# Two steps of ScalarE reordered, the router's product turned the other way, and five clears moved behind the selections, in a two-block transformer kernel

## What is computed

```python
# first block, each layer, after one wide projection of h
qkv_b = jax.nn.silu(causal_depthwise_conv(qkv_b, conv_w[layer]))
q_b, k_b, v_b = jnp.split(qkv_b, ...)
q_b = l2_normalize(q_b.reshape(B, S, GDN_HEADS, GDN_DK))   # x * rsqrt(sum(x*x) + eps)
k_b = l2_normalize(k_b.reshape(B, S, GDN_HEADS, GDN_DK))
o_b = chunked_gated_delta_rule(q_b, k_b, v_b, beta, g)
...
# second block, layer 1, after its attention mixers
c = rms_norm_2(h, norm_ffn[i])
h = h + moe_swiglu(c, moe_router[0], ...)   # logits = c @ router (1024 x 8), 2 of 8 experts a token
gate = jax.nn.sigmoid(rms_norm_2(h, ple_norm[i]) @ ple_w_gate[i])
h = h + (p[i] @ ple_w_proj[i]) * gate
```

## Time and profile before

| | |
|---|---|
| three runs | 2664.57, 2675.79, 2676.34 us; median 2675.79 |
| profiled execution | 2670.33 us, of which the span from first to last instruction is 2668.8 us |
| granted TensorE clock, mean | 0.965 |
| TensorE busy | 2564.6 us, 96% of the span |
| ScalarE busy | 493.8 us, 19% |
| VectorE busy | 637.0 us, 24% |
| read from HBM | 538.12 MB, 202 GB/s over the span |

### The profile page before, as it was taken

How to read it: one execution, slowest core, us unless ns; L and a number is a source line. 1 busy time by engine, 2 the same in 40 slices (tenths; PEclk the granted TensorE clock), 3 DMA queues, 4 the chain that set the end, 5 groups by cost and what they waited for, 6 DMA issues and landing times. The chain is left out here.

```text
span 2668.8 us, 47414 instructions
## 1 busy us (share of the span) xinstructions
PE 2564.6 (96%) x21427; PEld 1435.9 (54%) x21427; DVE 637.0 (24%) x1337; ACT 493.8 (19%) x847; POOL 133.8 (5%) x331
## 2 busy tenths in 40 slices
PE   9999999989999998999999988999999999999998
PEld 8666557756554774444445765353444535353444
DVE  3433532433543532000014443010101001010102
ACT  1521321422322432001013430000000000000001
POOL 4011000011000310000001300000000000000000
PEclk9998998999999988999999888999999999999999
DMA  7421333421335412444346213999999999999991
GB/s 242 130 76 53 111 116 126 142 80 64 105 108 131 147 41 91 142 154 145 134 136 163 82 42 144 370 367 380 356 386 345 375 364 370 373 363 378 358 368 66
DMA packets 192349, 542.29 MB, mean 203 GB/s; under 512 B 29168, under 2 KB 57232, under 8 KB 192144
## 3 DMA queue, kind: packets, MB, share of 16 engines
q1 hardware_dynamic: 178848, 536.95, 55.9%
q10 hardware_dynamic: 12992, 1.22, 0.4%
q0 software_dynamic: 304, 1.05, 0.1%
HBM read 538.12 MB, written 1.05 MB: 202 GB/s over the span
## 5 line engine op out<-in xcount | busy, mean ns | idle before, releaser
L398 PE MATMUL psum<-ring,hT 128*128 128x512 f32 (+3 forms) x1632 | 693.6, 583 | 19.2 <-ACT area L736 13.2
L398 PEld LDWEIGHTS psum<-ring,hT 128*128 128x128 f32 x1632 | 312.3, 199 | 359.7 <-issue 328.1
L2594 PE MATMUL psum<-ring,area 128*32 128x448 f32 x4608 | 439.5, 539 | 1.7 <-DVE area L2767 1.1
L2594 PEld LDWEIGHTS psum<-ring,area 128*32 128x32 f32 x4608 | 149.9, 110 | 283.8 <-issue 281.3
L623 PE MATMUL psum<-hT,ring 128*128 128x256 f32 x768 | 170.6, 385 | 0.0
L623 PEld LDWEIGHTS psum<-hT,ring 128*128 128x128 f32 x768 | 148.8, 194 | 21.7 <-issue 1.0
L2613 PE MATMUL psum<-area 128*32 128x256 f32 x2688 | 149.8, 380 | 2.0 <-ACT area L2743 2.0
L2613 PE MATMUL psum<-ring,area 128*32 128x256 f32 x2688 | 151.5, 380 | 0.0
L2594 PE MATMUL psum<-area 128*32 128x448 f32 x1536 | 147.3, 539 | 0.0
L2613 PEld LDWEIGHTS psum<-area 128*32 128x32 f32 x2688 | 85.7, 110 | 60.2 <-ACT area L2743 3.9
L2613 PEld LDWEIGHTS psum<-ring,area 128*32 128x32 f32 x2688 | 84.9, 110 | 57.1 <-issue 2.9
(11 more groups left out here) (528 smaller groups left out, 2362.7 us busy)
## 6 DMA issues: line engine op xcount, KB each, us to landing
ring<-in_w_in_dram SPq DMA_DIRECT2D x92, 1024.0 KB, 5.1
ring<-in_moe_w_gate_dram SPq DMA_DIRECT2D x96, 896.0 KB, 6.8
ring<-in_moe_w_up_dram SPq DMA_DIRECT2D x96, 896.0 KB, 7.8
area<-in_moe_w_down_dram SPq DMA_DIRECT2D x112, 512.0 KB, 7.4
ring<-in_moe_w_down_dram SPq DMA_DIRECT2D x112, 512.0 KB, 6.9
area<-in_moe_w_gate_dram SPq DMA_DIRECT2D x32, 896.0 KB, 6.7
area<-in_moe_w_up_dram SPq DMA_DIRECT2D x32, 896.0 KB, 8.0
ring<-in_w_out_dram SPq DMA_DIRECT2D x16, 1024.0 KB, 5.0
```

The costliest lines, as they stand in the source:

```text
L398: last = nc.tensor.matmul(acc(g)[:, t, 0:d["n"]], lhs(kk, t), w[:, k, :], start=kk == 0, stop=kk == d["nk"] - 1)
L2594: last = nc.tensor.matmul(PS[32 * j:32 * j + 32, 3 * p + b, 0:PIECE], XG[:, k, 32 * b:32 * b + 32], expert_slot(j0 + j // 2, GROUP * (j % ...
```

## The change

It has three parts, and each has something moved or replaced. `proj1_act` calls `rsqrt(1, p1)`, which copies p1's tile out between Ln and Exp, in both layers of the first block. `pass_act` issues the dummy activation with Sqrt and the read of the count between the last two copies, and `norm_act` leaves its own out for n=8; the branch for the extra passes ends with a Sqrt of its own. In the routing the router's columns are the weights and HT moves through, VectorE copies the 8 x 256 result out, TensorE transposes its two halves, and one copy brings both out; `clear_dve` stands behind the weighed selections.

```diff
-            rsqrt(1)
-            next(p1)
+            rsqrt(1, p1)
             next(p1)
             conv_silu(5)
...
             s.after(...ACT.Ln, bias=eps, scale=scale)...
+                if p1 is not None:
+                    next(p1)
             s.after(...ACT.Exp, scale=-0.5)...
...
+        def root_table(s):
+            s.do(nc.scalar.activation(WARM, ONES[:, 0:1], ACT.Sqrt))
...
-            s.do(nc.scalar.activation(WARM, ONES[:, 0:1], ACT.Sqrt))
+            if n != 8:
+                root_table(s)
...
                 s.after(nc.scalar.activation(PR[:, 0, 0:512], PS[:, 3, :], ACT.Copy)...
+                root_table(s)
+                count = busiest(act)
                 act.wait_ge(sem("weights_used"), used(MOE1))
                 s.after(nc.scalar.activation(PR[:, 1, 0:512], PS[:, 0, :], ACT.Copy)...
+                return count
...
-                for t in range(T):
-                    last = nc.tensor.matmul(PS[:, 2 * t, 0:NE], ht_lhs(k, t), ROUTER[:, k, :],
-                                            start=k == 0, stop=k == KD - 1)
+                last = nc.tensor.matmul(PS[0:NE, 0, 0:S], ROUTER[:, k, :], HT[:, k, :], start=k == 0, stop=k == KD - 1)
+            last.then_inc(signal("moe_rows"), 1)
+            pe.wait_ge(signal("moe_rows_out"), reached("moe_rows_out", 1))
+            for t in range(T):
+                last = nc.tensor.transpose(PS[:, 2, t * NE:(t + 1) * NE], LOGR[:, t * P:(t + 1) * P], IDENT[0:NE, 0:NE])
...
-            clear_dve()
+            s.eng.wait_ge(signal("moe_rows"), reached("moe_rows", 1))
+            s.after(nc.vector.tensor_copy(LOGR, PS[0:NE, 0, 0:S]).then_inc(signal("moe_rows_out"), 1), "moe_rows_out")
             s.eng.wait_ge(signal("moe_logits"), reached("moe_logits", 1))
-            for t in range(T):
-                s.do(nc.vector.tensor_copy(LOGX[:, t, 0:NE], PS[:, 2 * t, 0:NE]))
+            s.do(nc.vector.tensor_copy(LOGX[:, :, 0:NE], PS[:, 2, 0:2 * NE].rearrange("p (t e) -> p t e", t=T)))
...
             ins.then_inc(ms("weighed"), 1)
+            clear_dve()
             s.eng.wait_ge(ms("YE"), 3 + past("YE", r))
```

More of the change, by code:

```diff
@@ L84, in blocks_kernel @@
             "dsa_by_vector": ("dsa_kms", "dsa_roped"),
-            "route_by_vector": ("moe_mask", "moe_shifted", "moe_count"),
-            "route_by_tensor": ("moe_logits", "moe_places"),
+            "route_by_vector": ("moe_rows_out", "moe_mask", "moe_shifted", "moe_count"),
+            "route_by_tensor": ("moe_rows", "moe_logits", "moe_places"),
         }
@@ L649, in conv_silu, with rsqrt @@
                 s.do(nc.scalar.activation(Y[:, 4 * j:4 * j + 4, :], Y[:, 4 * j:4 * j + 4, :], ACT.Silu))
-            def rsqrt(hq):
+            def rsqrt(hq, p1=None):
                 if L + hq == 0:
@@ L2420, in blocks_kernel @@
         IOTA = iota_t[:, 0:CAP]
+        LOGR = view(14728, S)[0:NE]
         MORE = AREA - (MOE_RING - RING * HALF)
@@ L2553, in pass_dve @@
                     s.after(ins.then_inc(ms("placed"), 1), "moe_placed")
-            if r:
-                clear_dve()
-            else:
+            if r == 0:
                 shares_dve(s)
@@ L3061, in _, with second @@
                     s.after(nc.scalar.activation(EXPL, EXPL, ACT.Exp).then_inc(sem("moe_exp"), 1), "moe_exp")
-                    pass_act(s, 0)
-                    overflow(act, lambda: (pass_act(s, 1), pass_act(s, 2)))
+                    count = pass_act(s, 0)
+                    def second():
+                        for r in (1, 2):
+                            pass_act(s, r)
+                        nc.scalar.activation(WARM, ONES[:, 0:1], ACT.Sqrt)
+                    overflow(act, second, count)
                 norm_act(s, n)
```

## The result

The changed kernel takes 2654.78 us (median of 8 runs, 2650.74 to 2660.51), the kernel before 2674.75 (8 runs, 2664.57 to 2676.34). The ratio is 0.9933, 95% interval 0.9917 to 0.9949: faster by 14 to 22 us. The profiled execution of the changed kernel has a span of 2650.0 us against 2668.8, and a mean clock of 0.971 against 0.965.

A forecast was written before the change was run, and what follows sets the result against it. TensorE, busy 96% of the span, was taken as the bound, so time comes from its idle stretches and low clock. Terms of 11.7 + 3.2 + 0.3 = 15.2 us, against a mean of 2671.8, gave 2657 us; range 2647 to 2669.

The forecast's parts named there:

- The copy between Ln and Exp: First projection, both layers: TensorE restarts 3.1 us earlier in each, clock stays up for 5.5 us more; 11.7 us gained.
- Late Exp: First projection: k's product comes later, slack shrinks from 8 to 1.4 us but holds; as rival, 2660 us, chance 0.05.
- The Sqrt table and the count: Last norm: table load and count read leave the path, 2.15 us of wait and 1.0 of clock; 3.2 us gained.
- drain of the table load: Last norm: alternative reading of the 1.25 us ahead of the table load, which would give 2.7 us instead of 2.15.
- The router: Routing: sixteen records of 256 columns take 5.8 us instead of 6.99, less a new round trip; 0.3 us gained.
- The round trip: Routing: new PSUM copy, two transposes and hand-overs cost 0.6 to 1.0 us net, taken as 0.9.
- The place products: Routing: 2.30 us at clock 0.50 could become 1.15 if the clock is up.
- the middle case: Routing: sum of the middle terms, a gain of 0.3 us, between a loss of 0.9 and a gain of 3.6.
- The clears: Routing: 2.2 us of clears now lie in the gather's shadow, still covered, by 0.6 us.
- The clock does not come back: Rival: TensorE restarts earlier in both layers but the clock falls or later stages lose it; 7.5 us, 2664; chance 0.22.
- More than forecast: Rival: clock up through router, places and last norm; 20 us gained, 2652 us; chance 0.10.
- Slower, by the transfers of the experts: Rival: expert transfers fall below 362 GB/s and set the pace; at 3% less, 14 us slower, 2686; chance 0.05.

The follow-up runs named there:

- e1: The kernel before with only the copy of p1's tile moved between Ln and Exp; ratio 0.9950 (0.9932 to 0.9967).
- e5: The kernel before, copy still behind Exp, with four unused products of 512 columns in TensorE's wait for that copy; ratio 0.9980 (0.9968 to 0.9992).
- e2: The changed kernel with the copy of p1's tile back behind Exp; ratio to before 0.9989 (0.9972 to 1.0006).
- e4: The kernel before with only the turned router and the clears behind the selections; ratio 0.9998 (0.9981 to 1.0014).
- e6: The changed kernel with two extra 128x2048 copies on ScalarE between the copy of p1's tile and Exp; ratio to before 0.9974 (0.9959 to 0.9988).
- e8: The changed kernel with unused TensorE products in routing and last-norm waits, and first-pass clears behind the first scaling of gathered tokens; ratio to before 0.9919.
- e3: The kernel before with only the Sqrt table and the read of the count ahead of the last copy; ratio 0.9999 (0.9983 to 1.0016).
- e9: The changed kernel itself, run once more on one chip beside the kernel kept busy in its waits; ratio to before 0.9934, median 2652.99 us.
- e7: The changed kernel with the five clears back ahead of the wait for the router's rows; ratio to before 0.9925 (0.9904 to 0.9946).
- e10: The kernel of e8 run once more, beside e9 on the same chip; ratio to before 0.9931, median 2651.81 us.

## Why the prediction was right, point by point

**The copy between Ln and Exp: right, step and size.** Forecast 3.1 us of wait a layer and 2.4 and 3.1 us of clock, 11.7 in all. The trace has 3.06 (4.24 to 1.18) and the distances 5.40 and 6.07, 11.5 in all; e1 alone gives 11.5, e5 the clock's 5.3. That the clock's part came out so near to 5.5 is partly luck of the trace that it was read from: e2 puts it at 4.1 us and e4 at 4.7. The step that mattered was to take the clock's part from an idle time of the same length in the same stage, and to count it at all: with the wait alone I would have forecast a difference too small to tell.

**Late Exp: right.** Forecast slack 1.4 us. VectorE's product ends at 131.13, and the products that wait for it begin at 132.54, 1.4 us later; e6 puts the slack at 1.5 us.

**The Sqrt table and the count: the mechanism right, two sizes a little off.** Forecast 2.15 us of wait, measured 2.62: I gave ScalarE's branch the 0.67 us of VectorE's, and it needs 0.22. VectorE's 0.67 still stands in the changed kernel, so it is not a measure of the branch on another engine. The clock's part was 0.6 us, not 1.0: the idle time of 2.64 us left the clock up for L596 (0.71 us instead of 1.22), and it fell all the same soon after. It is 1.00 until 2614.40 and 0.52 from there to 2617.60, so that L2331's four records take 2.80 us and the first run of L398 14.72 us, where e8 has 1.88 and 13.90. The two errors cancel almost wholly in the sum of this part, 3.2 us both forecast and measured. In the trace of e3 the sum of both stretches is the same 17.70 us, with the low stretch on L2330 instead. The reading of 1.25 us as a drain of the table load, for which the Trainium skill ("ScalarE: Activation LUTs", section "What ACT_TABLE_LOAD costs") gives about 1380 ns, is refuted here by e3's rows: moved, the load begins 0.01 us after the copy, and nothing of the kind is ahead of it or behind. The size of the gain could not have told, for 2.62 us is nearer to the 2.7 us that the prediction worked out for the drain than to its own 2.15. No run moved the load and the read of the count one without the other; that the 1.25 us was the read follows since nothing else was left there.

**The router: right in sum, from terms that went up and down.** The records took 5.67 us against a forecast of 5.8, and the clock did rise while they ran (0.50 from 1626 to 1628 us, 0.99 from 1628 to 1630). The round trip: from the records' end to MAX8 it was 0.44 us before and is 1.17 in the changed kernel (1630.71 less 1629.54), 0.7 us more against a forecast of 0.9. The place products ran at full clock, from the mask to the selections 2.05 us instead of 3.06, 1.0 us gained where I had counted on none in the middle case. And the gather lost 0.75 us, which I had not foreseen: the low level began later and lasted into it (0.50 from 1636 to 1640 us, 0.57 from 1640 to 1642). In sum 0.87 us gained, forecast 0.3. That the sum came so near is thus owed to two terms that cancel, the place products and the gather, neither of which the middle case had. The clears were covered, by 1.5 us; with the gather at its old 5.80 us it would have been 0.7, about the 0.6 of the forecast. With the gather at e8's 3.81 us they would have held up the scaling by about 1.4 us: its weighed selections end at 1637.6, the clears take 2.2, and the scaling starts at 1638.4 there.

**The sum.** Forecast 15.2 us, measured in the touched parts 15.6. The other 3.2 us of the span come from stretches that the change leaves alone, and are within what these differ by between two executions of one kernel. They belong to no term of the forecast. The medians are 20 us apart, the means of the same runs 18, and the interval reaches down to 14, so the 15.2 us of the forecast lie inside it. That the whole came out clear of noise is right, but the forecast lay only 1.8 us above its own bound for that, and chance helped. In e9 the touched parts are 16.1 us shorter than before and the span only 10.6. The level of 2657 us is 2 us from the measured 2654.78, because the kernel before was put at 2671.8 us and its eight runs have a median of 2674.75.

**The rivals.** "The clock does not come back" fell with e1, e2 and e5. "More than forecast" came true for the place products only: the clock was low at the start of the router and behind the last norm, and it took e8's unused products to keep it up there. "Slower, by the transfers of the experts" did not occur: the experts' first record to the last norm's transposes is 964.94 us in both kernels. Its threshold was worked out wrong: a gain of 15.2 us is 1.6% of 961 us, not 1.4%, which changes nothing else.

**Left open.** What sets the clock in the first 20 us of an execution was not tried, nor what sets it in the long stretch between the second layer's place and the router. Nor was it tried whether unused products in the mixers, where the clock is 0.84, would give more than the routing's 4 us.

## What to carry to other kernels

When TensorE waits for one engine's list to reach a copy, look for the long pass that stands ahead of the copy and has slack of its own, and price the move as wait plus the clock behind it: here 6.1 and 5.3 us of 11.5, the second figure less sure than the first, since other traces of the old order give 4.1 and 4.7. Test the clock's part by filling the wait with unused products, which leaves the wait and removes the idle time. A gain below half a per cent in a kernel of this length shows in the distances between rows of a trace and not in the total, for the clock of untouched code moves the total by several us from one execution to the next.

## What the runs showed of the hardware that was not expected

- The same start of the program ran at clock 0.56 in one execution and 1.00 in another (10 to 20 us), 4 us apart at 118 us. The granted clock can miss such a stretch: e8's window says 1.00, while its first 32 records of L398 take 7.10 us (before: 6.70, e7: 4.22).
- The clock can fall after TensorE has restarted, and the length of the idle time alone does not decide it near 2.5 us: of two waits of 2.37 us in the same execution (e6), one was followed by clock 0.50 and one by 1.00. Behind 2.64 us (changed, e3) the next four records still ran at 1.00, and the clock fell 0.6 to 1.4 us after the restart. Idle times of 1.17 us left it up in all seven traces that have them at the first place.
- With the clock at 1.00 throughout the routing (e8, e10), the router's sixteen records took 4.24 us, about as long as VectorE's scaling of HT, which feeds them (4.12 us for eight blocks).
- Reading a word from memory into a register and branching on it cost ScalarE 1.25 us in the path; read earlier, the branch left 0.22 us (e3).
